# Hybrid decoder step on one core: first transfers reordered, output slices halved around the prompt's attention, the last V tile bank by bank

## The reference

```python
h = rms_norm(x, norm1_g)
z = h @ w_in                      # split: u 512, q 512, k 128, v 128, iq 512, ik 64, iw 8
q, k = rope(rms_norm(q)), rope(rms_norm(k)); iq, ik = rope(iq), rope(ik)
ya = pool_mix(u)                  # windows 2/4/8/16, per-group linear
score = sum_h relu(iq_h . ik) * iw_h      # indexer; causal; top 64 (prompt) or 256 (sample) keys
yb = softmax(q . k over the chosen keys) @ v
x = x + concat([ya, yb]) @ w_o
h2 = rms_norm(x, norm2_g)
x = x + peer(h2)                  # product-key retrieval over 128 x 128 experts, 8 heads x 16
```

## Time and profile before

| | |
|---|---|
| median of 3 runs | 1041.75 us (1040.34 to 1044.41) |
| profiled execution | 1040.79 us, its span 1039.1 us |
| PE matmul / weight load busy | 98% / 82% of the span |
| DVE / ACT / POOL busy | 69% / 50% / 44% |
| chain that ended last, by engine | PE 80%, DVE 9%, issue 4%, POOL 3%, ACT's queue 2% |
| DMA | 237.39 MB, mean 228 GB/s |

### The profile page before, as it was taken

How to read it: one execution, slowest core, us unless ns; L and a number is a source line. 1 busy time by engine, 2 the same in 40 slices (tenths; PEclk the granted TensorE clock), 3 DMA queues, 4 the chain that set the end, 5 groups by cost and what they waited for, 6 DMA issues and landing times.

```text
span 1039.1 us, 18875 instructions
## 1 busy us (share of the span) xinstructions
PE 1018.1 (98%) x6303; PEld 848.5 (82%) x6303; DVE 716.8 (69%) x1510; ACT 519.2 (50%) x1083; POOL 452.7 (44%) x329
## 2 busy tenths in 40 slices
PE   5999999999999999999999999999999999999998
PEld 2447878889999999999999988888878887778886
DVE  2559989649999728787888876764555555555553
ACT  2123222343445567777777775644444454444542
POOL 4653443245688878778887771011111111111110
PEclk9999999999999999999999999999999999999999
DMA  9434469358755578888888876675666766676662
GB/s 341 114 122 158 151 203 337 119 203 292 268 177 183 171 236 286 287 279 289 287 292 272 288 232 226 230 270 194 228 224 235 240 228 223 227 239 234 228 227 100
DMA packets 79439, 237.39 MB, mean 228 GB/s; under 512 B 11749, under 2 KB 23661, under 8 KB 78980
## 3 DMA queue, kind: packets, MB, share of 16 engines
q1 hardware_dynamic: 65052, 195.51, 55.4%
q0 software_dynamic: 13040, 40.52, 12.2%
q10 hardware_dynamic: 1280, 0.53, 0.2%
HBM read 233.56 MB, written 3.14 MB: 228 GB/s over the span
## 4 chain that ended last, share of the span: by engine, by line
PE 80%; DVE 9%; issue 4%; POOL 3%; ACTq 2%; DMA 1%; ACT 0%; SPq 0%; POOLq 0%; DVEq 0%
PE psum L1058 33%; PE psum L988 14%; PE psum L993 10%; PE psum L992 6%; PE psum L1004 5%; POOL w_lo L1521 3%; DVE top L1625 3%; DVE work_s L1626 2%; PE psum L580 2%; PE psum L819 2%; PE psum L1089 2%; PE psum L792 1%; ACTq L366 1%; ACTq L363 1%; PE psum L762 1%
## 5 line engine op out<-in xcount | busy, mean ns | idle before, releaser
L1521 POOL TENSOR_TENSOR w_lo<-w_raw,w_hi 128x1024 fp32r<-128x1024 f32 x116 | 285.6, 2467 | 95.1 <-ACT w_hi L1110 92.2
L1110 ACT ACTIVATE w_hi<-w_raw 128x1024 fp32r<-128x1024 f32 x214 | 227.4, 1063 | 175.6 <-PE psum L1058 95.4
L993 PE MATMUL psum<-h_split,w_lo 128*128 128x256 f32 x1024 | 287.6, 281 | 0.0
L988 PE MATMUL psum<-h_split,w_hi 128*128 128x512 f32 x640 | 232.1, 403 | 0.0
L993 PEld LDWEIGHTS psum<-h_split,w_lo 128*128 128x128 f32 x1024 | 194.6, 190 | 0.0
L1549 POOL DMA_INDIRECT rows_in<-expert_v,eidx x32 | 45.5, 1421 | 329.6 <-PE psum L1089 317.6
L1877 DVE TENSOR_TENSOR w_lo<-w_raw,w_hi 128x1024 fp32r<-128x1024 f32 x98 | 120.1, 1225 | 78.5 <-ACT w_hi L1110 78.5
L1058 PE MATMUL psum<-w_hi,ag_hi 128*128 128x512 f32 x512 | 160.1, 394 | 0.3 <-DVE ag_lo L1884 0.3
L1058 PE MATMUL psum<-w_hi,ag_lo 128*128 128x512 f32 x512 | 158.2, 390 | 0.0
L992 PE MATMUL psum<-h_split,w_hi 128*128 128x256 f32 x768 | 140.4, 285 | 1.3 <-issue 0.9
L988 PEld LDWEIGHTS psum<-h_split,w_hi 128*128 128x128 f32 x640 | 120.4, 188 | 25.5
(11 more groups left out here) (294 smaller groups left out, 1413.6 us busy)
## 6 DMA issues: line engine op xcount, KB each, us to landing
w_raw<-expert_ut SPq DMA_DIRECT2D x128, 512.0 KB, 4.7
w_raw<-expert_v SPq DMA_DIRECT2D x86, 512.0 KB, 3.9
raw_more<-expert_v SPq DMA_DIRECT2D x42, 512.0 KB, 4.1
w_slice<-w_pq_cols SPq DMA_DIRECT2D x32, 512.0 KB, 6.2
rows_in<-h_save SPq DMA_DIRECT2D x32, 512.0 KB, 4.5
w_most<-w_in_blocks SPq DMA_DIRECT2D x8, 699.0 KB, 12.3
w_slice<-w_o_half SPq DMA_DIRECT2D x8, 512.0 KB, 4.3
v_cache<-cache_v POOLq DMA_DIRECT2D x64, 64.0 KB, 2.9
```

What stands on the lines that cost most here:

```text
L988: pe.matmul(psum[:, 2 + s, :], w_hi[:, s, c, :], h_split[:, c].rearrange("p a t -> p (a t)"), start=(c == 0), stop=False, skip_group_check ...
L993: mm = pe.matmul(out, w_lo[:, s, c, :], h_split[:, c, 0], start=False, stop=(c == KC - 1), skip_group_check=wide)
L1110: return act.activation(out, in_, ACT.Copy)
L1521: pool.tensor_tensor(w_lo[:, s], w_raw[:, s], w_hi[:, s].bitcast(F32), ALU.subtract).then_inc(S["w_lo_ready"], 1)
```

## The change

Four edits, in no loop of the kernel:

1. SP loads only the first piece of `xT` ahead of the first block of `w_in`, the other three behind it, and `ident` behind the last block.
2. POOL issues the gains ahead of the page table. Then it waits for the fourth block of `w_in` (`w_in_in3` at 32) ahead of `early_loads`, and so ahead of all that stands behind them. ACT waits for the same block ahead of its 16 pages.
3. In the prompt's part PE takes two of unit 7's eight steps ahead of `prompt_heads(1)`; `wo_first(0)` takes its second chunk first and waits for the pooling groups one by one; the slices 2 and 3 are taken as halves on both sides of `prompt_values(0)` and `prompt_values(1)`.
4. For the last V tile the three terms of each bank follow each other, so that bank 0 is complete after 3 of 12 matmuls, bank 1 after 6, bank 2 after 9.

```diff
@@ SP @@
-            for k in range(0, KC, 2):
+            def load_x(k):
                 sp.dma_start(xT[:, k:k + 2, :], x_t[:, k:k + 2, :]).then_inc(S[f"x_in{k // 2}"], 16)
-            sp.dma_start(ident[:], c_ident).then_inc(S["ident_in"], 16)
+
+            load_x(0)
             for k in range(KC):
                 sp.dma_start(w_most[:, k], w_in_blocks[k, :, 0:3, :]).then_inc(S[f"w_in_in{k}"], 16)
                 sp.dma_start(w_rest[:, k], w_in_blocks[k, :, 3, :]).then_inc(S[f"w_in_in{k}"], 16)
+                if k == 0:
+                    for c in range(2, KC, 2):
+                        load_x(c)
+            sp.dma_start(ident[:], c_ident).then_inc(S["ident_in"], 16)
@@ PE @@
             prompt_idx(0)
+            z_prompt(7, 0, 2)
             prompt_heads(1)
-            z_prompt(7, 0, KC // 2)
+            z_prompt(7, 2, KC // 2)
...
-            def wo_first(q):
+            def wo_first(q, parts=(0, 1), ready=False):
 
                 slice_in(q)
-                for a in range(2):
+                for i, a in enumerate(parts):
                     c = CHUNKS[2 * q + a]
                     for k in range(4):
+                        if i == 0 and ready:
+                            pe.wait_ge(S["pool_y_copied"], k + 1)
...
-            pe.wait_ge(S["pool_y_copied"], NG)
-            wo_first(0)
+            wo_first(0, (1, 0), ready=True)
             prompt_logits(1)
             prompt_probs(0)
             wo_first(1)
+            wo_first(2, (0,))
             prompt_values(0)
+            wo_first(2, (1,))
             prompt_probs(1)
-            wo_first(2)
+            wo_first(3, (0,))
             prompt_values(1)
-            wo_first(3)
+            wo_first(3, (1,))
...
+                if last:
+                    low_in(NU + v)
+                    for i in range(len(Y_ORDER)):
+                        term(i, ag_hi[:, s, :], w_hi[:, s])
+                        term(i, ag_lo[:, v % 2, :], w_hi[:, s])
+                        term(i, ag_hi[:, s, :], v_low(v), stop=True).then_inc(S["y_psum"], 1)
+                    return
@@ ACT @@
             act.wait_ge(S["gains_in"], 16 * len(gain_loads))
+            act.wait_ge(S["w_in_in3"], 32)
             ik_loads(act, W_IK[0] + W_IK[1], W_IK[2])
@@ POOL @@
             for dst, src in gain_loads:
                 pool.dma_start(dst, src).then_inc(S["gains_in"], 16)
+            pool.wait_ge(S["w_in_in3"], 32)
             for dst, src in early_loads:
                 pool.dma_start(dst, src).then_inc(S["consts_in"], 16)
             pool.wait_ge(S["gains_in"], 16 * len(gain_loads))
             ik_loads(pool, W_IK[0], W_IK[1], "ik_in_pool")
```

More of the change, by code:

```diff
@@ L345, in hybrid_kernel @@
     v_rows = expert_v.rearrange("a (n p) d -> (a n) p d", p=P)
-    gain_loads = [(pages[0:1, :], page_table.rearrange("b n -> (b n)").unsqueeze(0)), (gains[:, :], gain_cols)]
+    gain_loads = [(gains[:, :], gain_cols), (pages[0:1, :], page_table.rearrange("b n -> (b n)").unsqueeze(0))]
     early_loads = [
@@ L764, in wo_first @@
                                        skip_group_check=True)
-                mm.then_inc(S["wo_half"], 1)
+                if len(parts) == 2 or parts[0] == 1:
+                    mm.then_inc(S["wo_half"], 1)
             def slice_in(q):
@@ L1068, in prod_v @@
                 for i in range(len(Y_ORDER)):
[L1069 to L1073, removed]
+                    mm = term(i, ag_hi[:, s, :], v_low(v))
+                mm.then_inc(S["prod_done"], 1)
             def residual():
```

## The result

The changed kernel takes 1050.13 us, the median of 4 runs (1049.12 to 1051.29), beside 1041.05 us for the kernel before (4 runs, 1040.03 to 1044.41). The ratio is 1.0084, with a 95% interval of 1.0063 to 1.0105: slower, by 9.1 us. The forecast was 1052.0 in a range of 1048 to 1056. The profiled execution took 1051.29 us, its span 1049.6, 10.5 us more than before's 1039.1.

What follows compares the result with a forecast made beforehand. DVE's rounds on `score_s` were taken to bound the start, with POOL's queue 0.8 us from delaying PE. +12.3 + 1.7 - 2.5 - 0.8 = +10.7 us on 1040.79 gave 1051.5, forecast 1052 us, range 1048 to 1056.

Steps and rivals of the forecast that it cites:

- POOL, predicted +12.3: POOL's wait for `w_in`'s fourth block delays its pages and `fold_iw`, so PE's unit 4 and all behind: +12.3 us.
- the lower bound: All favourable bounds together, including POOL's rotation at 5.7 instead of 6.8 us: +6.0 us, 1048 us in total.
- the slack of 0.8 us: Ahead of PE's first transposes, `fold_iw` was ready 0.8 us before DVE's rotation, which comes off POOL's delay.
- The clock, predicted +1.7: Behind PE's new pause of some 13 us the array runs at 1.2 GHz for a while: +1.7 us, bound 0.
- Edit 1 and ACT's wait, predicted 0: At the start, the first block lands some 3 to 4 us earlier, but queues of page loads keep their times: 0.
- Edit 3, predicted -2.5: In the prompt's part PE's pauses are filled and DVE's waits of 1.9 and 0.7 us go: -2.5 us.
- Edit 4, predicted -0.8: At the tail three stores are issued before the last bank's copy ends: -0.8 us, bounds -0.3 and -1.2.
- The signs to look for: Profile signs: POOL's first group at 23 to 25 us, last 50 to 52, `fold_iw` 60 to 61, `score_s` wait near 22.
- the one on the other side: POOL's pages go over 2 us a group faster, so PE doesn't wait for POOL: 1038 us or 1036, chance 0.05.
- No earlier block: `w_in`'s fourth block still lands near 19.0 us, making POOL later by another 2.5 us: 1054.5 us, chance 0.08.
- nothing of the shift was absorbed: Rival: part of the shift is absorbed between 60 and 192 us; with half absorbed 1046 us, chance 0.06.

Runs made afterwards that it cites:

- the smaller dose: Changed kernel with POOL waiting for the second block of `w_in` instead of the fourth, ACT still for the fourth: 1044.25 us, ratio 1.0021.
- The wait-free filler: Changed kernel with 15 more products into an unused PSUM bank, so PE works through nearly all of its pause: 1045.38 us, ratio 1.0045.
- the repeat: The changed kernel timed and profiled once more, unaltered, beside the kernel before: 1047.38 us, ratio 1.0070.

## Why the prediction was right

The sign and the chain were right: POOL's wait, its queue, PE's stop, the shift of `score_s` and the shift of the end. The experiment with the wait alone and the smaller dose show it. The number, 1052.0 against 1050.13, was closer than its terms: POOL's was 3.4 us too large, and late landings that no term held made up for about as much in the profiled execution. That closeness is luck. (Two slips of the working change nothing: 12.3 + 1.7 is 14.0 and not 13.9, and 1051.5 + 1.0 is 1052.5.)

- *POOL, predicted +12.3, measured +8.9.* This term was mis-sized, by three steps. The block landed at 15.83 rather than 16.5. The gap ahead of the first group was 2.48 us, since its wait for the gains had long been met, and I took 3.3. Above all, the rotation took 5.7 us instead of 7.6. I had put that only into the lower bound, at a part of its size. The constants' issue (3.9 us) and the pages (29.1 us) were as predicted, and so was the slack of 0.8 us.
- *The clock, predicted +1.7, measured +2.25* in the eight products. The wait-free filler gave 2.5 us back. The Trainium skill (TensorE: Matmul & The Clock Gate, "What's actually happening") has an idle array fall to 1.2 GHz and rise only after sustained work; the rows agree, with 0.50 granted behind the pause.
- *Edit 1 and ACT's wait, predicted 0.* Under POOL's wait this is right, to 0.0004 of the ratio. But I wrote that both paths "keep their times within a few tenths" and gave ACT 0.3 us were POOL's wait not there. That step failed: alone, ACT's wait costs 3.6 us, and edit 1 brings ACT's copy forward by 3 to 5 us (36.26 against 39.53 before and 40.91 with edits 3 and 4). ACT's queue of 16 pages sits directly ahead of that copy, just as POOL's sits ahead of the rotation, and it starts behind the first block, so an earlier block does move it. I priced one of the two queues.
- *Edit 3, predicted -2.5, measured -3.25 against the profile of before, -1.6 against two others.* The two waits went as written, 1.9 and 0.7 us. But the 1.9 was the low clock of that execution: without it DVE waits 0.2 us for the adds (POOL's wait alone). I took the 1.7 us of low clock for a fixed part of the kernel. The 0.7 beyond is DVE's: its three later pairs of adds took 0.67 us from the start of one to the next instruction instead of 0.90. So with PE ahead, a row that named no wait became shorter too.
- *Edit 4, predicted -0.8, measured -1.3.* The stores did spread, over 2.27 us, and the last was issued 1.4 us behind the last matmul's start instead of 2.3, which is the 0.9 that I had worked out as 0.8. The total is 0.1 beyond the bound of -1.2. The other 0.4 us lie behind it: from the last store's issue to the end of the span are 2.2 us instead of 2.6. The last copy ends 1.0 us behind the matmul's start as before, as predicted.
- *Not in the sum: late expert weights, 0 to 3.8 us.* Without them the measured terms add up to 8.9 + 2.25 - 3.25 - 1.3 = +6.6 us, 1047.4 us from the profile of before, and the repeat measured 1047.38, which is below my range. The range held the first measurement with the help of landings that it had not counted, as far as its one profiled execution (1051.29 us) tells; what the three others, 1049.12 to 1050.93 us, were made of was not profiled.
- *The signs to look for.* POOL's first pages came at 22.20, below the 23 to 25 written; its last ended at 51.3, inside 50 to 52; `fold_iw` at 57.1, below 60 to 61. DVE's wait near 22 us appeared as two, 12.6 and 11.6 us, because the prompt's rotation stood in the queue between them.

Of the rivals, the one on the other side asked for POOL's pages to go faster on emptier DMA: they took 5.33 us a group again. *No earlier block* was out by 3 us, and nothing of the shift was absorbed: 11.17 us at `score_s` less edit 3's 3.25 is the 7.9 at the mask. With POOL's wait alone 11.83 became 10.17, by the low clock that only before's profile had.

## What to carry to other kernels

A wait placed ahead of transfers in an engine's queue delays everything behind it there, the arithmetic too. Price it from the queue's next computation, and price every engine that gets such a wait on its own: under the dearest the others look free, and come out when that one is removed. When a change bundles edits, run the good ones without the rest; here two edits worth 3.4 us in the medians were hidden under a loss of 11 in the traces. Compare a stretch with more than one execution before pricing an edit on it: half of one edit's gain here was a clock that fell in one trace and not in two others. And moving a wait behind transfers that it was to hold back can give nothing, when these then delay what is waited for.

## What the runs showed of the hardware

**POOL's arithmetic depends on what DVE does.** The same six 32x288 operations took 0.78 to 0.81 us each while DVE stood still (the changed kernel), and up to 1.37 us while it worked (1.40 in the kernel before). The timeline of POOL without both waits, when DVE was rotating at the same time:

```profile
39.75 1.12 POOL L1491 TENSOR_TENSOR idx_tmp<-z,rope 32x288 f32<-32x288 f32 x1
...
45.25 1.37 POOL L1496 TENSOR_TENSOR z<-idx_tmp 32x288 f32<-32x288 f32 x1
```

DVE paid as well: its 32x320 instructions took 1.08 us each beside these, and 0.48 in the changed kernel with POOL only issuing. Who pays changes from row to row: DVE's product of z with the prompt's norms took 2.07 us in the changed kernel, while two of POOL's instructions beside it kept to 0.78, and 0.90 us before, where one of POOL's beside it took 1.26. The Trainium skill (SBUF — State Buffer, "SBUF: two separate sides") says that GpSimd shares a pair of ports with a DVE instruction that has two inputs in SBUF, as these have, and that the pair is a lock held for a whole instruction by whichever starts first. The rows agree in direction. By it a shift of one against the other changes both, which is what took 1.9 us off POOL's term.

**The granted clock fell also behind short pauses, but not always.** It fell behind 3.05 us (no POOL wait, 5.85 us for the eight products). Behind pauses of 1.23 us (edit 3 alone) and 0.99 us (edits 3 and 4) the eight products took 3.40 us, and behind one of 1.20 us with edit 4 alone they took 5.09, as the timelines of PE show, first of edit 3 alone:

```profile
49.06 0.49 PE L558 MATMUL psum<-ident,z 32*128 32x32 f32 x5 [1.23 <-DVE z L1622]
...
49.60 3.40 PE L580 MATMUL psum<-w_most,hT 128*128 128x466 f32 x8
```

and of edit 4 alone:

```profile
49.52 0.49 PE L558 MATMUL psum<-ident,z 32*128 32x32 f32 x5 [1.20 <-DVE z L1621]
...
50.07 5.09 PE L580 MATMUL psum<-w_most,hT 128*128 128x466 f32 x8
```

Up to there the programs of these three and of the kernel before are the same. With the low clock `score_s` came at 68.81 us, 2.9 later than before, 1.2 of them since the transposes were later and 1.7 by the clock. Around the prompt's values it was alike: behind pauses of 1.14 and 0.72 us the kernel before was granted 0.52, and the two other kernels with these pauses, POOL's wait alone and edit 4 alone, 1.00. So short pauses can cost 1.7 us in one execution and nothing in another, and one trace doesn't tell which is usual.
